# Token loads of a mixture-of-experts stage issued two blocks ahead instead of four

## The reference, cut to what matters

```
scores = sigmoid(xb @ router_w);  sel = scores + router_bias
group  = argmax over 4 groups of the sum of the group's top 2
e_idx  = top 2 experts of 16 inside that group; combine = their scores, normalised
hid    = silu(xb @ w_gate[e]) * (xb @ w_up[e])          # 1024 -> 256, per expert
out    = sum over e of combine[e] * (hid @ w_down[e])   # 256 -> 1024
x      = x + g2 * out
```

## Time and profile before

| | |
|---|---|
| three runs | 1272.78, 1272.94 and 1275.27 us; median 1272.94 us |
| the profiled execution | 1275.27 us, span 1273.1 us, mean granted clock of PE 0.878 |
| PE busy (matmul) | 993.4 us, 78% of the span |
| PE weight load | 667.3 us, 52% |
| DVE, ACT, POOL busy | 459.9, 321.4 and 87.9 us |
| DMA | 240.61 MB, 189 GB/s on the mean |

### The profile page before, as it was taken

How to read it: one execution, slowest core, us unless ns; L and a number is a source line. 1 busy time by engine, 2 the same in 40 slices (tenths; PEclk the granted TensorE clock), 3 DMA queues, 4 the chain that set the end, 5 groups by cost and what they waited for, 6 DMA issues and landing times. The chain is left out here.

```text
span 1273.1 us, 23862 instructions
## 1 busy us (share of the span) xinstructions
PE 993.4 (78%) x10201; PEld 667.3 (52%) x10201; DVE 459.9 (36%) x1283; ACT 321.4 (25%) x626; POOL 87.9 (7%) x148
## 2 busy tenths in 40 slices
PE   4999979698569769876399997959866976977751
PEld 2556566597345465533255655658734545643321
DVE  0213655765541321111321264676654133111113
ACT  1260245322510411101125124532241041101100
POOL 0000000000000022111100000000000002211121
PEclk7999979699679888999589997989977987999975
DMA  9598324400145289998722332240013218999963
GB/s 388 205 255 261 139 93 165 168 9 4 67 155 190 95 335 342 373 368 301 266 99 100 103 113 85 107 194 8 4 67 129 108 39 350 363 372 389 367 239 146
DMA packets 39762, 240.61 MB, mean 189 GB/s; under 512 B 5408, under 2 KB 5408, under 8 KB 16096
## 3 DMA queue, kind: packets, MB, share of 16 engines
q1 hardware_dynamic: 26784, 194.63, 40.6%
q0 software_dynamic: 12864, 44.32, 11.1%
HBM read 211.13 MB, written 27.79 MB: 188 GB/s over the span
## 5 line engine op out<-in xcount | busy, mean ns | idle before, releaser
L866 PE MATMUL bank<-sb_hT,sb_ring 128*128 128x385 f32 (+1 forms) x640 | 213.7, 494 | 4.4 <-ACT sb_hT L1418 4.4
L866 PEld LDWEIGHTS bank<-sb_hT,sb_ring 128*128 128x128 f32 (+1 forms) x640 | 121.1, 190 | 93.9 <-issue 13.9
L866 PE MATMUL bank<-sb_arena 64*64 64x64 f32 (+6 forms) x1064 | 114.4, 341 | 34.9 <-DVE sb_arena L1687 22.0
L1418 ACT ACTIVATE sb_arena<-bank 128x512 f32<-128x512 f32 (+4 forms) x122 | 53.3, 458 | 322.9 <-PE bank L866 255.3
L1418 ACT ACTIVATE sb_u<-bank 128x256 f32<-128x256 f32 (+2 forms) x92 | 41.6, 462 | 248.0 <-PE bank L866 247.4
L866 PEld LDWEIGHTS bank<-sb_arena 64*64 64x64 f32 (+2 forms) x1064 | 63.4, 147 | 69.8 <-issue 27.8
L866 PE MATMUL bank<-sb_ring,sb_arena 128*64 128x256 f32 (+1 forms) x536 | 79.5, 441 | 19.5 <-DMA sb_ring<-weights 15.6
L866 PE MATMUL bank<-sb_o,sb_ring 128*128 128x385 f32 x256 | 87.5, 505 | 8.0 <-issue 8.0
L1687 DVE TENSOR_TENSOR sb_arena<-sb_arena,bank 128x128 f32<-128x128 f32 (+1 forms) x91 | 26.0, 320 | 176.8 <-ACT sb_arena L1418 171.0
L1418 ACT ACT_TABLE_LOAD x61 | 78.3, 1283 | 3.4 <-DVE sb_scond L2279 1.2
L866 PE MATMUL bank<-sb_u,sb_arena 64*64 64x64 f32 (+2 forms) x784 | 62.8, 308 | 15.6 <-DMA sb_u<-weights 11.0
(11 more groups left out here) (177 smaller groups left out, 1179.8 us busy)
## 6 DMA issues: line engine op xcount, KB each, us to landing
sb_ring<-weights SPq DMA_DIRECT2D x117, 1024.0 KB, 9.0
sb_u<-weights SPq DMA_DIRECT2D x24, 1024.0 KB, 18.5
sb_arena<-weights SPq DMA_DIRECT2D x24, 1024.0 KB, 22.3
sb_arena<-x_slots POOLq DMA_DIRECT2D x39, 256.0 KB, 7.4
y_slots<-sb_arena POOLq DMA_DIRECT2D x70, 128.0 KB, 6.8
sb_sq<-weights SPq DMA_DIRECT2D x8, 1024.0 KB, 25.9
sb_hT<-weights SPq DMA_DIRECT2D x8, 1024.0 KB, 26.8
x_slots<-sb_arena POOLq DMA_DIRECT2D x1, 6912.0 KB, 40.1
```

Source lines behind the costliest of these rows:

```text
L866: return nc.tensor.matmul(out, lhsT, rhs, start=start, stop=stop, skip_group_check=True)
L1418: return nc.scalar.activation(out, in_, func, **kw)
```

## The change

The loads run two blocks ahead in the extra blocks. In the loop over blocks 0 to 15 the load of block b + 4 is issued only as long as b + 4 is below 18, so blocks 14 and 15 issue no load. In the loop over the extra blocks the load of block b + 2 (before: b + 4) is issued, inside the same branch. The waits of POOL for loads that nobody else waits for are taken out: in the changed kernel every load is waited for by PE.

```
                 for b in range(EXPERTS):
-                    if b + 4 < BLOCKS:
+                    if b + 4 < EXPERTS + 2:
                         load_tokens(b + 4)
                     store_block(b)
                 for b in range(EXPERTS, BLOCKS):
                     with pool.If(used > b):
-                        if b + 4 < BLOCKS:
-                            load_tokens(b + 4)
+                        if b + 2 < BLOCKS:
+                            load_tokens(b + 2)
                         store_block(b)
                 for b in (EXPERTS - 2, EXPERTS - 1):
                     wait_stored(pool, l, b)
-                for b in (EXPERTS + 2, EXPERTS + 3):
-                    pool.wait_ge(more_xb_loaded[l][b - EXPERTS - 2], 16)
                 for b in range(EXPERTS, BLOCKS):
                     with pool.If(used > b):
                         wait_stored(pool, l, b)
-                        if b + 4 < BLOCKS:
-                            pool.wait_ge(more_xb_loaded[l][b + 4 - EXPERTS - 2], 16)
```

## The result

| | before | changed |
|---|---|---|
| median of four runs | 1274.11 us (1272.78 to 1276.37) | 1286.22 us (1281.65 to 1287.31) |
| ratio | | 1.0094, 95% interval 1.0073 to 1.0115 |
| span of the profiled execution | 1273.1 us | 1283.6 us |
| mean granted clock of PE | 0.878 | 0.885 |

The forecast was +6.2 us and a range up to 1284.5 us; the kernel lost about twice that. (The kernel before was timed again beside each group of kernels; its median lay between 1274.1 and 1275.5 us.)

The account below looks back on a forecast made before the run. Bound: POOL's chain of waits in layer 1, from the last store to the first gather. Layer 0 -1.0 us plus layer 1 +7.2 us gave +6.2 on the 1272.94 us median: 1279.1 us, range 1274.0 to 1284.5.

Parts of the forecast that it names:

- three rounds through POOL: Layer 1's extra blocks: down, store, next load, landing, transposes, next down become a loop, each round 5.79 us plus the landing.
- store issue to load issue, with the branch: POOL, layer 1, each round: two store issues, 1.05 us, and one branch, 0.15 us, before the load.
- once more on top: Layer 1, PE at half clock for part of block 17: 1.5 us added once, bounds 0 and 3.7.
- The landings: Layer 1's three extra-block token loads, each right behind a store pair, take 7.8, 7.8 and 3.8 us to land.
- short landings: Rival, layer 1: loads land in 3.4 us despite weights in flight, only down(18) late; +1.2 us, 1274.1 us; chance 0.12.
- The weights add nothing: Layer 1: DMA engines keep bringing weights while PE stands, so a later PE finds them there; no added time.
- the first late round: Layer 1, block 16: down(16) starts at 1212.78 because of the wait for load 18, 2.75 us late.
- The layer 0 term: End of layer 0: without unused loads 18 and 19 the last store lands sooner; gather gains 1.0 us, bounds 0 to 1.4.
- The gap: Layer 1, POOL: the store's 1.29 us gap between its halves in block 16 may return and delay the load behind it.
- clock lost more widely: Rival, layer 1: blocks 16 and 17 both at half clock, store gap returns; +9.7 us, 1282.6; chance 0.20 including long landings.

Follow-up runs that it names:

- warm_pe_short: Changed kernel plus 12, 8 and 4 added matmuls of constants on PE ahead of its waits for the three token loads; 1.0077 of the kernel before.
- warm_pe: Changed kernel plus 20, 14 and 5 added matmuls of constants on PE ahead of its waits for the three token loads; 1.0058 of the kernel before.
- one_stall: Changed kernel with only load 18 left behind the previous block's store, loads 19 and 20 issued ahead of their block's store; 0.9993 of the kernel before.
- late_transposes: Changed kernel with PE's transposes of block b + 2 moved behind down(b) in the extra blocks; 0.9966 of the kernel before.
- l1_near: Kernel before with the changed order of loads in layer 1 alone; 1.0089 of the kernel before.

## Why the prediction was wrong, step by step

The direction and the place were right: layer 1 alone, three rounds through POOL, 35 loads, and PE's transposes released by the token load. The size was not. The forecast of the stage was 38.27 us for `down(15)` to `down(18)` (36.77 and 1.5 of clock), 2.96 to the store and, as before, 5.69 from there to the gather, 46.92 us in all; measured are 51.73. Term by term:

| term | forecast | measured | difference |
|---|---|---|---|
| load issue to PE's first transpose, three times | 7.8 + 7.8 + 3.8 = 19.4 | 9.12 + 6.12 + 3.30 = 18.54 | -0.9 |
| store issue to load issue, with the branch | 3 x 1.20 = 3.60 | 1.02 + 1.04 + 2.46 = 4.52 | +0.9 |
| half clock, transposes to down | 0 | 0.34 + 0.35 + 0.34 = 1.03 | +1.0 |
| half clock, down to store (over 2.96) | 1.5 | 1.69 + 1.78 + 1.75 = 5.22 | +3.7 |
| `down(18)`'s store to the gather | 5.69 | 5.69 | 0 |
| sum | | | +4.8 |

**The step that failed is the clock.** The forecast put 1.5 us "once more on top", for "part of that block", with 3.7 us as the upper bound; the trace has 6.25 us. Two errors are in it. I took only `down(17)` to pay, although the forecast's own rounds leave PE idle ahead of each of the three blocks; all three began at the half clock and had it through `down`. And I ended the count at the start of `down(18)`: that matmul and the way to its store are on the path too, 1.75 us. That the long idle time brought the half clock is shown as far as the traces go: in the changed kernel the clock fell inside each of the three waits, and with PE kept at work in warm_pe_short it was 1.00 in block 16, and `down(18)` to its store took 2.97 us. What idle time is short enough is not shown, for the clock also fell with PE at work behind shorter waits: in the kernel before at 1218 (1.09 and 2.06 us, for weights), in warm_pe (0.92 us) and in warm_pe_short (1.39 us).

**The landings** were right in sum by luck: the first was longer than taken, the second shorter. The "short landings" rival has fallen: 9.0 and 6.0 us with the weights in flight, 3.2 without. The Trainium skill, "DMA: Bandwidth & Descriptors", section "Queues, rings and completion order", has each DMA engine take turns between the queues, a packet each. The conclusion that the prediction drew from it for this rival, that about 3.4 us would do at any time, did not hold: 9.0 and 6.0 us.

**The weights.** "The weights add nothing" held for the whole loop. But one_stall shows more than that: they forgive. The forecast charged the first late round (2.75 us) like the others, and one_stall shows that it alone would have been made up but for 1.1 us of the stage. That the weights came out at nothing here is only because all three rounds are late and the loop, not the weights, sets the end.

**The layer 0 term**, -1.0 us, was too large: some 0.4 us in the traces, nothing that the time can tell. From the last half store (about 607.2 in the changed kernel) to POOL's first branch at 610.9 it still took some 3.7 us with no load ahead, and not 3.07. So the load ahead of it was at most a part of what made the store slow; the rest is open.

**The gap** of 1.41 us between the store pair and the load in block 17 was named as a possible addition and left out of the sum; it came, also in warm_pe, warm_pe_short and late_transposes.

**The range** ended 1.7 us short. 1.2 us of that is the base: it was drawn up from a median of 1272.94 us for the kernel before, which a fourth run moved to 1274.11. As a difference, it reached to +11.6 us, and measured are +12.1. The "clock lost more widely" rival (1282.6 us) was nearest, and it too counted two blocks only.

## What to carry to other kernels

In a queue that is in order, a prefetch is as late as the instruction that it stands behind: a load placed behind a store that waits for a result is no prefetch, even if its own buffer has long been free. Before moving one, write down the loop (result, store, load, landing, consumer, next result) and compare its length with what bounds the stage; in this stage, which waits for weights, a single late round cost 1.1 us and each further one 5 to 6. And when a stall leaves PE idle for several us (3.5 to 7.2 here), count the half clock for every block that follows such an idle time, up to and including the last one.

## What the runs showed of the hardware that was not expected

- The granted clock fell inside the waits, not at the same distance from their start: in the changed kernel some 5 us after PE's last work (1204.74, fall just before 1210), in l1_near between 1207 and 1208, some 2 us after it (1205.47). It came back to full with PE at work, near 1216.7 in the changed kernel. At half clock eight matmuls of `down` took 3.68 us against 1.94, and the way from down to store 4.7 against 2.96.
- A token load of 256 KB, right behind a store pair and with weights in flight, took 8.9 to 9.5 us from issue to landing in the first round, 5.5 to 6.4 in the second, and 3.0 to 3.4 in the third, with the weights in, in the changed kernel, l1_near and the two warm kernels.
- A matmul call with 128 columns of constants as weights and 256 columns of data took 0.44 us (20 in 8.90, at a granted clock of 1.00), where one of `gate_up`, with 64 columns of weights and the same 256 of data, took 0.24 us (8 in 1.95). The calls of `gate_up` also write the two halves of the bank in turn, so which of the two differences counts is not shown.
